# Eight gate stores of a hybrid decoder step, issued by SyncE in place of ScalarE

## The reference, cut to what matters

```
x  = x + 1/2 SwiGLU(RMSNorm(x))
h  = RMSNorm(x)
a, b, q, k, v, qi, ki, wi, gc, ga = split(h @ w_in)
u  = a * sigmoid(b)
conv = silu(LayerNorm(depthwise_conv31(u))) @ w_cout
att  = sparse_attention(q, k, v; top-k keys chosen by qi, ki, wi)
x  = x + (sigmoid(gc) * conv + sigmoid(ga) * (att @ w_aout)) @ w_o
x  = x + 1/2 SwiGLU(RMSNorm(x))
```

## Time and profile before

| | us |
|---|---|
| median of 3 runs | 1515.6 (1514.41 to 1520.02) |
| profiled execution, its own time | 1529.38 |
| its span, first to last instruction | 1527.6 |
| PE busy in it | 1433.8 (94%) |
| DVE / ACT / POOL busy | 1045.1 / 546.0 / 590.3 |

### The profile page before, as it was taken

One profiled execution on the slowest core, in us unless ns is written; L12 is line 12 of the kernel. 1 busy time (PEld: TensorE's weight loads), 2 busy tenths in 40 slices (PEclk: granted clock), 3 DMA queues, 4 the chain that ended last, 5 costly groups with the idle time before them and its releaser, 6 DMA issues. The chain is left out here.

```text
span 1527.6 us, 20866 instructions
## 1 busy us (share of the span) xinstructions
PE 1433.8 (94%) x8219; PEld 1125.7 (74%) x8219; DVE 1045.1 (68%) x1684; ACT 546.0 (36%) x838; POOL 590.3 (39%) x415
## 2 busy tenths in 40 slices
PE   4998999989899999999989899999998999999998
PEld 2333578767788876446766565689998999999998
DVE  1256688987727698989796998667669756664221
ACT  2332556324622232031112233453364444453211
POOL 2000474444269855634326676323203553420000
PEclk8999999999999999999999999999999999999999
DMA  9996263312157887958427876432332223312222
GB/s 346 361 381 229 85 105 100 93 59 83 56 158 231 280 279 246 333 161 300 149 83 250 285 239 194 155 139 84 124 97 69 84 83 111 98 45 74 89 86 88
DMA packets 156931, 248.77 MB, mean 163 GB/s; under 512 B 11965, under 2 KB 104909, under 8 KB 156571
## 3 DMA queue, kind: packets, MB, share of 16 engines
q1 hardware_dynamic: 131742, 164.22, 33.5%
q0 software_dynamic: 23104, 76.16, 15.9%
q10 hardware_dynamic: 1989, 7.07, 1.2%
HBM read 237.58 MB, written 10.20 MB: 162 GB/s over the span
## 5 line engine op out<-in xcount | busy, mean ns | idle before, releaser
L2783 POOL TENSOR_TENSOR w_lo<-w_raw,w_hi 128x1024 fp32r<-128x1024 f32 x65 | 169.8, 2612 | 235.9 <-ACT w_hi L1330 235.3
L696 PE MATMUL ps<-bh,wqr 128*128 128x288 f32 x936 | 205.3, 295 | 4.2 <-DVE wqr L1939 1.9
L2850 POOL DMA_INDIRECT kv<-cache_v,idxT x128 | 136.5, 1067 | 102.1 <-PE ps L1108 50.6
L1330 ACT ACTIVATE w_hi<-w_raw 128x1024 fp32r<-128x1024 f32 (+1 forms) x88 | 91.2, 1037 | 234.4 <-PE ps L647 161.7
L2838 POOL DMA_INDIRECT kv<-cache_k,idxT x128 | 140.2, 1095 | 88.3 <-DVE kprod L2473 56.4
L696 PEld LDWEIGHTS ps<-bh,wqr 128*128 128x128 f32 x936 | 155.5, 188 | 5.0 <-DVE wqr L1939 3.8
L647 PE MATMUL ps<-h_hi,w_hi 128*128 128x512 f32 x352 | 140.8, 400 | 7.5 <-DVE xT L2273 4.5
L647 PE MATMUL ps<-h_hi,w_lo 128*128 128x512 f32 x352 | 138.5, 394 | 0.0
L647 PE MATMUL ps<-h_lo,w_hi 128*128 128x512 f32 x352 | 138.5, 393 | 0.0
L712 PE MATMUL ps<-a_hi,wqr 128*128 128x288 f32 x704 | 122.3, 295 | 0.0
L1093 PE MATMUL ps<-h,wn 128*128 128x288 f32 x448 | 115.2, 416 | 5.6 <-issue 2.0
(11 more groups left out here) (513 smaller groups left out, 3177.8 us busy)
## 6 DMA issues: line engine op xcount, KB each, us to landing
w_raw<-w_ffn_in SPq DMA_DIRECT2D x56, 512.0 KB, 12.5
wq<-w_ffn_in SPq DMA_DIRECT2D x40, 512.0 KB, 3.6
wn<-w_in SPq DMA_DIRECT2D x36, 512.0 KB
qb<-q_scratch SPq DMA_DIRECT2D x64, 256.0 KB
ring<-w_ffn_in SPq DMA_DIRECT2D x28, 512.0 KB
w_raw<-w_ffn_out SPq DMA_DIRECT2D x24, 512.0 KB, 9.7
wq<-w_ffn_out SPq DMA_DIRECT2D x20, 512.0 KB
ring<-w_ffn_out SPq DMA_DIRECT2D x14, 512.0 KB
```

The lines of the kernel that those rows point to most:

```text
L696: mm = pe.matmul(ps[:, bank + m, 0:HALF], w[:, k, m * P:(m + 1) * P], b[:, j, k, :], start=(j in (0, 1, 5) and k == 0 and fst), stop=(k == ...
L1330: act.activation(w_hi[:, slot, 0:n], w_raw[:, slot, 0:n], ACT.Copy).then_inc(S_("hi_ready"), 1)
L2783: pool.tensor_tensor(w_lo[:, slot, 0:n], w_raw[:, slot, 0:n], w_hi[:, slot, 0:n].bitcast(F32), ALU.subtract)\
L2850: pool.indirect_dma_start(kv[:, V_SLOT[j % 3] + a // 2, a % 2, :], None, rows[1], bass.IndirectOffsetOnAxis(ap=idxT[:, j % 2, t:t + 1], ax ...
```

## The change

`save_gate` moves, with the same waits, from ACT's program to SP's. ACT no longer issues the eight stores. SP issues store i of gates 0 to 4 ahead of the load of unit 30 + 2i, store 5 and store 6 ahead of the two waits for the first `w_aout` loads, and store 7 behind its wait for all units and ahead of the read-back.

```diff
+            def save_gate(i):
+
+                if i < 3:
+                    sp.wait_ge(S_("sgb_ready"), i + 3)
+                    sp.wait_ge(S_("mix_free"), i + 3)
+                else:
+                    sp.wait_ge(S_("gate_taken"), 4 * (i - 2))
+                sp.dma_start(gate_dram[i:i + 1, :, :].rearrange("o p n -> p (o n)"), sgb[:, :, :].rearrange("p m n -> p (m n)"))\
+                    .then_inc(S_("gate_saved"), 16)
...
+                if n >= 6 and n % 2 == 0:
+                    save_gate(n // 2 - 3)
                 native_load(m, win_v[:, 4 * (m % 2):4 * (m % 2) + 4, col:col + 256], 1024)
...
+            save_gate(5)
             sp.wait_ge(S_("ring_used"), N_RING + 35)
             load(UM, va[:, :, 0:256], 0, 1024)
+            save_gate(6)
             sp.wait_ge(S_("ring_used"), N_RING + 38)
             load(UM + 1, va[:, :, 256:512], 1, 1024)
             sp.wait_ge(S_("ring_used"), N_RING + NATIVE)
+            save_gate(7)
...
                 sigmoid(0, ACT.Tanh, 0.5)
-                save_gate(i)
...
-                if q % 4 == 3:
-                    save_gate(i)
```

More of the change, by code:

```diff
@@ L1714, in _ @@
             qk_root(1)
[L1715 to L1723, removed]
             def state_evac():
```

## The result

After the change the kernel takes 1534.45 us in the median of 6 runs (1527.99 to 1536.77), the kernel before 1518.57 us beside it (6 runs, 1514.41 to 1521.48). The ratio is 1.0098, 95% interval 1.0073 to 1.0122: slower by some 15 us, where the forecast had 5.6. The forecast was 1521.2, with 1527 as the top of its range, both counted from a median before of 1515.6. The profiled execution after took 1536.77 us, its span 1535.0.

The account below looks back on a forecast made before the run. PE, busy 94%, was taken to bound the kernel, with DVE as full around 850 us. The sum was 0 (ACT) + 0 (covered loads) + 5.6 = 5.6 us, so 1515.6 + 5.6 = 1521.2 us; range 1514 to 1527.

Parts of the forecast that it names:

- what costs nothing: ACT's eight dropped issues (2.6 us in all) and the later, covered loads on SP were each put at 0 us.
- the chain from DVE to PE: Late tap 0 delays DVE's reciprocals, then ACT's scaling and tanh, then PE's third quarter of gate 3, by 7.3 us.
- D: DVE's delay at convolution tap 0, waiting for the twelve prompt stores to land; taken as 10 us, with 4.6 and 13.8 kept.
- 2.65 us to spare: Slack of PE's third quarter of gate 3 behind ACT's tanh; PE would be late there by D - 2.65 = 7.3 us.
- second value: D of 9.4 us: prompt stores, unit 34 and the gate store ahead of them drain at q1's earlier 0.224 MB/us.
- The third bound in the prediction: All 3.28 MB drain beside POOL's gathers at 0.17 MB/us, taking 19.3 us from 850.5; D = 13.8 us.
- lowest bound: Twelve prompt store issues end at about 856.5 and land 4.1 us after the last, at 860.6; D = 4.6 us.
- 4.35 us to spare at the second place: Slack between ACT's tanh, ending 885.7, and PE's quarter at 890.05; PE's loss there 10 - 4.35 = 5.6 us.
- PE gets something back: PE's 3.54 us gather wait at 876.63 would be used up, cutting its first delay from 7.3 to 3.8 us.
- I count nothing for it: PE's clock would fall after a 7 us stall, as it fell to 0.83 in 870:880 before; put at 0 us.
- All of it is kept: Rival: D of 12 to 14 us, gather wait not given back, PE loses 9.4 to 11.2; 1525 to 1527 us; chance 0.28.
- Hidden: Rival: prompt stores land by 861, D under 5, gather wait swallows PE's first delay, 0.6 us left; 1516 us; chance 0.22.

Follow-up runs that it names:

- E2: The changed kernel with gate 2's store alone back on ACT, the other seven staying on SP; ratio 1.0011 to the kernel before.
- E4: The changed kernel with gate 2's store back on ACT, but SP still waiting for gate 2's tanh ahead of unit 34; ratio 1.0100 to the kernel before.
- E5: The changed kernel with all eight gate stores on SP, but the twelve prompt stores issued ahead of gate 2's store; ratio 0.9993 to the kernel before.
- E7: The changed kernel with nine of the twelve prompt stores issued ahead of gate 2's store and three behind it; ratio 1.0055 to the kernel before.
- E6: The changed kernel without the four v prompt stores (1.05 MB), that output left unwritten; ratio 1.0068 to the kernel before.
- E3: The kernel before with gate 2's store alone moved to SP, ahead of the load of unit 34; ratio 1.0106 to the kernel before.
- E8: The changed kernel run and profiled once more, nothing altered, beside E5 on the same chip; 1530.29 us.
- E9: The changed kernel with POOL also waiting, ahead of one group of value gathers, until the twelve prompt stores have landed; ratio 1.0078 to the kernel before.
- E1: The kernel before, profiled once more with nothing altered; 1528.38 us, beside a median of 1531.16.

## Why the prediction was wrong

**Right: what costs nothing.** ACT's eight issues gave nothing, and the seven other moved stores cost nothing (E2). The prompt stores behind SP's wait are the term that counts (E4 against E2, and E5 against the changed kernel).

**Right: the chain from DVE to PE.** PE's wait is D less 4.2 to 5.0. "PE late at q6" is taken at the second place where PE leans on DVE, the third quarter of gate 4 (q = 6): the time from the start of gate 3 to there, less the same time in E5 (879.85 - 844.89).

| run | D us | PE's wait | D less the wait | PE late at q6 | D less that | ratio |
|---|---|---|---|---|---|---|
| E7 | 7.77 | 3.35 | 4.42 | 7.1 | 0.7 | 1.0055 |
| E6 | 11.20 | 7.05 | 4.15 | 10.4 | 0.8 | 1.0068 |
| E4 | 13.89 | 9.46 | 4.43 | 13.1 | 0.8 | 1.0100 |
| E3 | 14.98 | 10.48 | 4.50 | 14.3 | 0.6 | 1.0106 |
| after | 15.85 | 11.40 | 4.45 | 15.0 | 0.8 | 1.0098 |
| E8 | 16.68 | 11.72 | 4.96 | 15.8 | 0.9 | |

The prediction had 2.65 us to spare. The measured 4.4 or so contains them: DVE's masks end 4.6 us behind gate 3's start (852.69 less 848.08) where it was 5.4 in the earlier trace rows, and PE had idled 1.6 us for a gather where it had idled 0.6. Both only shift who is waited for.

**Wrong: the size of D.** This is the first of the two terms of the sum that failed: D was taken as 10, "next to the second value", and came out at 15.85. The working behind it was a drain of 3.28 MB at 0.224 MB/us, the rate of q1 in 838:850. That rate held in a stretch where the gathers moved little. ("All had landed at about 850" is also some 1 us early: q1 still moved 40 packets, 0.02 MB, in 850:851.) The queues of the kernel before in 838:850:

```profile
q1 hardware_dynamic: 2236, 2.69, 66.0%
q0 software_dynamic: 354, 1.18, 31.0%
```

After the change, in 848:868, the gathers on q0 moved 3.56 MB in 20 us, 0.178 MB/us against 0.098, and q1 got 3.75 MB, 0.188 MB/us, most of unit 35's load (issued at 857.11) in it. The time from the first prompt store to tap 0 was 868.54 - 848.13 = 20.4 us, where my value of D meant 15.5. The third bound in the prediction, 0.17 MB/us with the gathers running all through, gave 19.3 and was nearly right. E9 settles the cause: the same bytes with most of the gathers held take 11.5 us. So gathers beside the stores are worth 9 of the 15.85 us. The other kernels line up roughly behind it: 2.69 MB took 19.0 us (E4, its gate store in ACT's queue not counted), 2.23 MB 15.9 (E6), 1.65 MB 12.4 (E7). About 5 us per MB and some 4 us over fit these, but for 1.5 us in E4; what the 4 us are no run shows. The prediction's lowest bound had 4.1 us from the last issue to landing. From the last prompt store's issue to tap 0 the changed kernel took 12.0 us (868.54 - 856.51), E7 10.5 and E9 3.6, so that term held only where the gathers were held.

The Trainium skill, "DMA: Bandwidth & Descriptors", section "Queues, rings and completion order", says that each DMA engine goes round the queues with work, one packet at a time. With it the prediction had noted that D would lie above its second value, 9.4, and then took 10. The trace shows near even bytes, 3.75 MB and 3.56 MB, but not an even count of packets as the profile counts them, 2872 and 1087; so it bears out the sharing and not the turn by packets.

**Wrong: 4.35 us to spare at the second place.** This is the other term of the sum that failed. The sum was D - 4.35, with 4.35 read from ACT's tanh at 885.29 and the quarter at 890.05. But PE came late to that quarter in the execution before: it had waited 3.54 us at 876.63. In E5, where PE's only wait between the start of gate 3 and there is 1.33 us, the tanh and the quarter are nearer:

```profile
878.75 0.69 ACT L1787 ACTIVATE sgb<-ps 128x288 f32<-128x288 f32 x2
```

The first of these two (0.39 us) ends at about 879.1, and the quarter starts at 879.85: 0.7 us to spare. All six profiles with the stores held bear it out: PE is late there by D less 0.6 to 0.9, and the loss by the ratio lies within some 2 us of that (the table). With D = 15.85 and 0.8 in the prediction's sum PE loses 15.0 us, and the ratio 1.0098 is 14.9 us. Of the 9.4 us that the forecast lacked, D made 5.85 and the spare time some 3.6.

**Wrong: "PE gets something back", 3.5 us.** The wait for a gather at 876.63 did vanish, but another of 1.60 us stands ahead of gate 3's third quarter (2.00 in E8, 1.33 in E5), and the wait that vanished was 1.56 us in E1 and not 3.54. The prediction set a single execution's wait against the median; that execution lay 13.8 us above it. It also let PE be held at the end only by the second place, D - 4.35, in the belief that the first loss would partly be returned. The first loss was 11.4, and nothing up to the second place returned any of it: there PE waited 0.24 us more (0.70 in E8).

**The clock, "I count nothing for it".** It fell, but up to the second place it made no part of the loss. The sixteen matmuls after the wait took 7.12 us in place of 4.15, 3.0 us; in E8 6.62, and 5.84 once more at 911.50. Even after a wait of 3.35 us (E7) it was 5.96, 1.8 us:

```profile
858.47 5.96 PE L1234 MATMUL ps<-h,wn 128*128 128x288 f32 x16 [3.35 <-ACT sgb L1791]
```

Yet at the second place PE is late by D less 0.7 in E7 and by D less 0.8 in the kernel after: had the quarter run in 4.15 us, PE would have waited there for ACT that much longer. So to count nothing was right for this stretch, though the reason given was not this one. Only behind it, in E8 at 911.50 (and in E4 at 913.58, 5.76 us), does a second slow quarter add something of its own.

**Where the time goes in E8, against E5.** Up to the second quarter of gate 4: the wait 11.72, the clock 6.62 - 4.15 = 2.47, the gather 2.00 - 1.33 = 0.67; together 14.9 of the 15.2 measured. From there to the second quarter of gate 5: the waits for late DVE and ACT at 895.81 (0.70) and 909.59 (1.05) and the clock at 911.50 (5.84 - 4.15 = 1.69), 3.4, of 3.1 measured. Afterwards E8 gets 3.5 us back, 1.2 of it the gather wait at 905.55 that only E5 has, and 0.8 a shorter wait for ACT at 1001.72 (0.87 against 1.67). The rest of the give-back was not traced.

**The rivals.** "All of it is kept" came nearest: no wait given back, but its D of 12 to 14 was still too small, and it took PE's loss as D - 2.65 where in the end it was D - 0.8. ("Hidden" gave PE's first delay as 2.2 us or less for a D under 5; 5 - 2.65 is 2.35.) "Hidden" leaned on the sentence of the Trainium skill ("DMA: Bandwidth & Descriptors", "Issuing engines are not separate DMA queues") that the issuing engine decides only the sequencer's issue time. E4 is against reading it so: there the issuing engine of every store is as in E2, and one wait on SP ahead of thirteen transfers costs 1%.

## What to carry to other kernels

A DMA that is moved to another engine's instruction stream brings its wait with it. List everything that is issued behind that wait, and for each the first instruction that needs its data. A store whose only reader seems to be memory can still be needed soon, by whoever overwrites its source: here twelve output stores held DVE's next write.

For how long transfers take to drain, don't take a queue's rate from a stretch in which the other queues were quiet. Use the rate beside the traffic that will run at the new time. Where bounds differ by a factor of three, ask which of them has the right neighbours before taking the middle one.

Spare time between two engines is only what it is when neither is held up by something else. Here 4.35 us were read from an execution in which PE itself had been waiting; without that wait 0.7 were left, and DVE's whole delay but 0.8 us came through. The slow clock behind a wait of PE (1.8 to 3.0 us for sixteen matmuls) cost nothing while the late engine was still the one to be waited for at the next meeting point.

## What was not expected of the hardware

With only three prompt stores, a load and the gate store behind the hold (1.65 MB), D was still 7.77 us (E7). The DMA engines were full, gathers among the traffic (397 GB/s in 850:856, DMA share 1.05), and even a small batch was slow: unit 35's 512 KB load, issued right behind the last store at 845.51, took 12.9 us to land there, and 4.5 us in E9 with the gathers held.

```profile
850.00:856.00 6.00, 3.39 (x24) 1.02 (x22) 0.76 (x2) 0.00 (x0) 4.25 (x6) 0.95 1.05 397
```
